# Routing of a mixture-of-experts layer: the row table built earlier, and GpSimd as a second engine for block 0's weight splits

## The chip, the cores and the metric

The kernel runs on one core of one Trainium2 chip. The metric is the device time of one execution in microseconds. The core has five engines that run their own instruction streams and wait for each other through semaphores: TensorE (PE; matmul, with its weight loads as PEld), VectorE (DVE), ScalarE (ACT), GpSimd (POOL) and SyncE (SP; it only issues DMAs here). GpSimd issues the indirect DMAs of this kernel.

## What is computed

One layer of a diffusion backbone: two token mixers, then a mixture of experts over 1024 tokens with 16 experts, and a final norm. The change touches the experts' part. Its reference, cut down:

```python
weights = grp_p * top_p / jnp.sum(top_p, axis=-1, keepdims=True)     # two experts for each token
expert = grp * EXPERTS_PER_GROUP + top_i
# assignments sorted by expert, each expert's segment padded to 128 rows: "blocks"
row_tok = jnp.full((n_rows,), n_tok, jnp.int32).at[dest].set(st)      # which token a row holds
row_w = jnp.zeros((n_rows,), jnp.float32).at[dest].set(sw)            # its weight
block_e = jnp.minimum(jnp.searchsorted(pad_end, jnp.arange(n_blocks) * MOE_BLOCK, side='right'), N_EXPERTS - 1)

def expert_block(args):
    xb, e = args
    gate, up = jnp.split(xb @ w_up[e], 2, axis=-1)
    return (jax.nn.silu(gate) * up) @ w_down[e]

y_rows = lax.map(expert_block, (x_rows, block_e)).reshape(n_rows, d)
y = jnp.zeros((n_tok + 1, d), h.dtype).at[row_tok].add(y_rows * row_w[:, None])
```

## The kernel before

`experts` (L2540) first computes the routing, then runs 31 blocks (BLOCKS) of 128 rows. All times below lie in its part of the span, from about 1692 us on.

Products are done in pairs of parts: a 32-bit matrix `raw` is split into `hi` (a rounded copy, made by ScalarE) and `lo` = raw - hi (VectorE, L2948), and a product is three matmuls, hi x hi, lo x hi, hi x lo (L2739 to L2741). An expert's weights come as three pieces of 128x4096 (q = 0, 1 for w_up, q = 2 for w_down), each split in two halves of 128x2048. A piece is loaded by GpSimd with an indirect DMA, `load(b, q)` (L2680), as soon as `lo_done[q]` says that the block before has been split; block 0 always takes expert 0, so its three pieces are loaded by SyncE at the start (L2650). ScalarE makes the hi halves of block 0's pieces 0 and 1 at L2801. VectorE makes the four lo halves at L2948, called as `split_lo(0, 0)` and `split_lo(0, 1)`.

The routing is done by VectorE in small instructions that each wait for the one before (helper `then`). After L2900 to L2909 it knows each assignment's place. For each of the two choices k it makes `hit` (L2913), `in_block` (L2914) and `is_rank` (L2915), which count up the semaphore `places`. TensorE multiplies them into `table_ps` (L2725): for each row of each block its token. VectorE then makes, in this order:

- the weight parts: `hit` times weight (L2918), and a split into two parts (L2920, L2921), which TensorE multiplies into `h_ps` (L2731): the weight of each row;
- each block's expert: le (L2924), reduce (L2926), min (L2927);
- the row numbers `w_rows` from which the experts' weights are loaded (L2929 to L2935);
- the table of tokens: `filled` (L2937), `row0` (L2938), `table` (L2939), and `target` (L2942), where the results are added.

GpSimd waits for `table` with its first two gathers of rows of x (L2688), then goes on to `load(1, 0)`. TensorE transposes the gathered rows (L2749, `turn_x`), ScalarE makes their hi part (L2814), VectorE the rest (L2953, `x_lo`), and the products of block 0 begin (L2739). VectorE's order behind the routing is `split_lo(0, 0)`, `x_lo(0)`, `split_lo(0, 1)`, then the row weights (L2986, L2987) and the loop over the blocks.

Two more instructions elsewhere serve the prediction as samples. L937 and L2213 are subtractions of GpSimd with two SBUF inputs, the same operation as L2948. L1254 and L1270 are VectorE instructions of a token mixer: L1254 reads a PSUM tile, L1270 two SBUF tiles. L2335 is a VectorE instruction on 8 elements with both inputs in SBUF.

Of the kernel before, what the change touches and what calls it, by code (L numbers as in the profile page):

```python
# [29 lines left out]
P = 128  # L30
# [864 lines left out]
class GateUnits:  # L895
# [21 lines left out]
    def load(self, sp, g):  # L917
        if g >= UNITS:
            return
        if g >= 2:  # L920
            sp.wait_ge(self.lo_done, g - 1)
        col = self.GATE_COLS[g // KD] + g % KD * P
        sp.dma_start(self.raw[:, g % 2, :, :], self.wsrc[:, :, col:col + P]).then_inc(self.w_loaded[g % 2], 16)
# [1616 lines left out]
def experts(nc, m, sem, w):  # L2540
# [10 lines left out]
    with ExitStack() as ctx:  # L2551
# [48 lines left out]
        blk = sb("rt_blk", [P, BLOCKS])  # L2600
        again = sb("rt_again", [P, BLOCKS])
        row0 = sb("rt_row0", [P, BLOCKS])
        part = sb("rt_part", [P, 4])
        filled = sb("rt_filled", [P, BLOCKS])
        spare = lo[:, 2, :]
# [23 lines left out]
            "loaded", "hi_done", "lo_done", "made"))  # L2629
        gathered = [sem(f"ex_gathered{j}") for j in range(2)]  # L2630
        gate_loaded, added, tabled = sem("ex_gate_loaded"), sem("ex_added"), sem("rt_tabled")
        block = ctx.enter_context(nc.Block())

        up_rows = w["w_up"][0].rearrange("e (p h k) n -> (e p h) (k n)", h=2, k=KQ)
# [3 lines left out]
        def each(eng, body):  # L2638

            for b in range(BLOCKS):  # L2640
                body(b, b % 2, b // 2)
        late = lambda b, n: b >= n
        more = lambda b: b < BLOCKS - 1

# [10 lines left out]
        @block.gpsimd  # L2655
        def _(pool):
            pool.iota(rank[:, :], pattern=[[1, P]], base=0, channel_multiplier=0,
                      allow_small_or_imprecise_dtypes=True).then_inc(built, 1)
            pool.iota(token[:, :], pattern=[[P, N]], base=1, channel_multiplier=1,
                      allow_small_or_imprecise_dtypes=True).then_inc(built, 1)  # L2660
            pool.iota(which[:, :], pattern=[[1, WIDE]], base=0, channel_multiplier=0,
                      allow_small_or_imprecise_dtypes=True).then_inc(built, 1)
            pool.iota(rank4[:, :], pattern=[[-1, 4]], base=4, channel_multiplier=0,
                      allow_small_or_imprecise_dtypes=True).then_inc(built, 1)
            pool.memset(ones16[:, :], 1.0).then_inc(built, 1)
            pool.memset(again_n[:, :, 0:1], 0.0).then_inc(built, 1)
            pool.memset(again_n[:, :, 1:N], 1.0).then_inc(built, 1)
            pool.iota(part[:, 0:2], pattern=[[1, 2]], base=0, channel_multiplier=2,
                      allow_small_or_imprecise_dtypes=True).then_inc(part_built, 1)
            pool.iota(part[:, 2:3], pattern=[[0, 1]], base=0, channel_multiplier=1,  # L2670
                      allow_small_or_imprecise_dtypes=True).then_inc(part_built, 1)
            pool.iota(part[:, 3:4], pattern=[[0, 1]], base=SEQ, channel_multiplier=1,
                      allow_small_or_imprecise_dtypes=True).then_inc(part_built, 1)
            pool.memset(again[:, :], 0.0).then_inc(part_built, 1)

            def load(b, q):

                pool.wait_ge(lo_done[q], 2 * b)
                rows = EXPERTS * P * (1 if q == 2 else 2)
                pool.indirect_dma_start(out=raw[:, q, :], out_offset=None, in_=sources[q],  # L2680
                                        in_offset=bass.IndirectOffsetOnAxis(ap=w_rows[:, q, b:b + 1], axis=0),
                                        bounds_check=rows - 1, oob_is_err=False).then_inc(loaded[q], 16)

            def gather(b):
                pool.wait_ge(tabled, 1)
                if b >= 2:
                    pool.wait_ge(s["t_x"], b - 1)
                pool.indirect_dma_start(out=xg[:, b % 2, :], out_offset=None, in_=m.h2,  # L2688
                                        in_offset=bass.IndirectOffsetOnAxis(ap=table[:, b:b + 1], axis=0))\
                    .then_inc(gathered[b % 2], 16)  # L2690
            def add(b):

                pool.wait_ge(tabled, 2)
                pool.wait_ge(s["y_left"], b + 1)
                if b:
                    pool.wait_ge(added, 16 * b)
                pool.indirect_dma_start(
                    out=m.x1, out_offset=bass.IndirectOffsetOnAxis(ap=target[:, b:b + 1], axis=0),
                    in_=yo[:, b % 2, :], in_offset=None, compute_op=ALU.add).then_inc(added, 16)
            gather(0)  # L2700
            gather(1)
            for b in range(BLOCKS):
                if b + 1 < BLOCKS:
                    load(b + 1, 0)
                    load(b + 1, 1)
                if b:
                    load(b, 2)
                if b + 2 < BLOCKS:
                    gather(b + 2)
                if b >= 2:  # L2710
                    add(b - 2)
            add(BLOCKS - 2)
            add(BLOCKS - 1)
            pool.wait_ge(added, 16 * BLOCKS)

        @block.tensor
        def _(pe):
# [7 lines left out]
                    last = pe.matmul(table_ps[:, 0:WIDE], is_rank[:, k, n, :], in_block[:, k, n, :],  # L2725
                                     start=(k == 0 and n == 0), stop=(k == TOP_K - 1 and n == N - 1))
            last.then_inc(tables, 1)
            pe.wait_ge(places, TOP_K + 1)
            for k in range(TOP_K):
                for n in range(N):  # L2730
                    last = pe.matmul(h_ps[:, 0:2 * WIDE], is_rank[:, k, n, :],  # L2731
                                     part_w[:, k, n, :, :].rearrange("p q b -> p (q b)"),
                                     start=(k == 0 and n == 0), stop=(k == TOP_K - 1 and n == N - 1))
            last.then_inc(tables, 1)

            def product(dst, a_hi, a_lo, q, at, k, first, last):

# [5 lines left out]
            def turn_x(b, j, half):  # L2743
                pe.wait_ge(gathered[j], 16 * half + 16)
                if late(b, 1):
                    pe.wait_ge(s["x_lo"], b)
                by_chunk = xg[:, j, :].rearrange("p (c k) -> p k c", k=KD)
                for k in range(KD):
                    last = pe.transpose(x_ps[:, k * P:(k + 1) * P], by_chunk[:, k, :], m.ident[:, :])  # L2749
                last.then_inc(s["t_x"], 1)  # L2750
# [12 lines left out]
            def step(b, j, half):  # L2763
# [21 lines left out]
                    last = pe.transpose(h_ps[:, k * P:(k + 1) * P], by_chunk[:, k, :], m.ident[:, :])  # L2785
                last.then_inc(s["t_h"], 1)
            turn_x(0, 0, 0)
            each(pe, step)
            down(BLOCKS - 1, (BLOCKS - 1) % 2, (BLOCKS - 1) // 2)

# [40 lines left out]
        def _(dve):  # L2831
            count = [0]

            def then(ins):
                count[0] += 1
                ins.then_inc(routed, 1)
                dve.wait_ge(routed, count[0])
# [74 lines left out]
            for k in range(TOP_K):  # L2912
# [1 line left out]
                then(tt(in_block[:, k], hit[:, k], wide(token[:, :], WIDE), ALU.mult))  # L2914
                tt(is_rank[:, k, :, :], wide(where[:, 0, k, :], P), along(rank[:, :], P), ALU.is_equal)\  # L2915
                    .then_inc(places, 1)
            for k in range(TOP_K):
                then(tt(hit[:, k], hit[:, k], wide(weight[:, k, :], WIDE), ALU.mult))  # L2918
            for k in range(TOP_K):
                then(dve.tensor_copy(part_w[:, k, :, 0, :], hit[:, k]))  # L2920
                then(tt(part_w[:, k, :, 1, :], hit[:, k], part_w[:, k, :, 0, :].bitcast(F32), ALU.subtract))  # L2921
            dve.sem_inc(places, 1)
            dve.wait_ge(part_built, 4)
            then(tt(le[:, :, :], ends[:, :].rearrange("p (a e) -> p a e", a=1).to_broadcast([P, BLOCKS, E]),  # L2924
                    which[:, 0:BLOCKS].rearrange("p (b a) -> p b a", a=1).to_broadcast([P, BLOCKS, E]), ALU.is_le))
            then(dve.tensor_reduce(blk[:, :], le[:, :, :], AX.X, ALU.add))  # L2926
            then(ts(blk[:, :], blk[:, :], float(E - 1), None, ALU.min))  # L2927

            then(tt(again[:, 1:], blk[:, 1:], blk[:, 0:BLOCKS - 1], ALU.is_equal))  # L2929
            then(ts(again[:, :], again[:, :], float(SKIP), None, ALU.mult))  # L2930
            for q, rows in enumerate((2 * P, 2 * P, P)):
# [1 line left out]
                    then(dve.scalar_tensor_tensor(out=row0[:, :], in0=blk[:, :], scalar=float(rows), in1=again[:, :],  # L2933
                                                  op0=ALU.mult, op1=ALU.add))
                then(ts(w_rows[:, q, :], row0[:, :], part[:, q:q + 1], None, ALU.add))  # L2935
            dve.wait_ge(tables, 1)
            then(ts(filled[:, :], table_ps[:, 0:BLOCKS], 0.5, None, ALU.is_gt))  # L2937
            then(tt(row0[:, :], table_ps[:, 0:BLOCKS], filled[:, :], ALU.subtract))  # L2938
            dve.tensor_copy(table[:, :], row0[:, :]).then_inc(tabled, 1)  # L2939
            then(ts(filled[:, :], filled[:, :], -1.0, 1.0, ALU.mult, ALU.add))  # L2940
            then(ts(filled[:, :], filled[:, :], part[:, 3:4], None, ALU.mult))
            tt(target[:, :], row0[:, :], filled[:, :], ALU.add).then_inc(tabled, 1)  # L2942

            def split_lo(b, q):
                for h in range(2):
                    at = slice(h * HALF, (h + 1) * HALF)
                    dve.wait_ge(hi_done[q], 2 * b + 1 + h)
                    dve.tensor_tensor(lo[:, q, at], raw[:, q, at], hi[:, q, at].bitcast(F32), ALU.subtract)\  # L2948
                        .then_inc(lo_done[q], 1)
# [13 lines left out]
            def step(b, j, half):  # L2963
# [15 lines left out]
                dve.tensor_tensor(ht_lo[:, :], h_ps[:, :], ht_hi[:, :].bitcast(F32), ALU.subtract)\  # L2979
                    .then_inc(s["h_lo"], 1)  # L2980
                split_lo(b, 2)
            split_lo(0, 0)
            x_lo(0)
            split_lo(0, 1)
            dve.wait_ge(tables, 2)
            then(dve.tensor_copy(row_weight[:, :], h_ps[:, 0:BLOCKS]))  # L2986
            then(tt(row_weight[:, :], row_weight[:, :], h_ps[:, WIDE:WIDE + BLOCKS], ALU.add))  # L2987
# [198 lines left out]
```

## Time and profile before

| | |
|---|---|
| median of 3 runs | 2354.45 us (2353.87 to 2356.31) |
| span of the profiled execution | 2351.6 us |
| busy: PE, PEld, DVE, ACT, POOL | 2150.2, 1736.6, 1410.3, 1025.9, 845.0 us |
| mean granted clock of TensorE | 0.957 |
| weight splits of VectorE (L2948) | 186 instructions, 416.1 us |

The profile lists instructions with their start from the beginning of the span and their duration. An instruction that is issued but can't proceed counts as running, so a duration above that of its like is a wait inside the instruction. Idle time before an instruction is given in brackets with what ended it. The granted clock is the share of full speed that TensorE was allowed; its two levels are 0.50 and 1.00.

### The profile page before, as it was taken

Reading aid. Unit: us, or ns where it says so; the run is one execution under the profiler, and the core shown is the slowest. Engines: PE = TensorE matmul, PEld = TensorE weight load, DVE = VectorE, ACT = ScalarE, POOL = GpSimd, SP = SyncE. Lnnn points to the kernel's source line nnn. Section 1 sums busy time; section 2 is a strip of 40 time slices with the busy share of each in tenths; the row PEclk is TensorE's granted clock in tenths of the full one; section 3 lists DMA queues with packets and bytes.
Section 4 is the critical chain, followed back from the end, with each engine's and each line's share of the span. In section 5 each row is a group of like instructions: output and inputs, shape, how many; then the busy total and the mean of one; then the engine's idle time right before and its main releaser. Section 6 shows DMA issues by size and latency. Waiting matters only on the chain. (4 is left out here: it accounts for less than half of the span.)

```text
span 2351.6 us, 26496 instructions
## 1 busy us (share of the span) xinstructions
PE 2150.2 (91%) x10128; PEld 1736.6 (74%) x10128; DVE 1410.3 (60%) x1688; ACT 1025.9 (44%) x1350; POOL 845.0 (36%) x614
## 2 busy tenths in 40 slices
PE   7999999998898995999999789999789999999992
PEld 1278878887787884888888667777667787877882
DVE  1549541100333324888988546345488899998993
ACT  2332311111234445556655334433246576666762
POOL 6300000111456654567766422210123444543531
PEclk9999999999999997999999999999889999999996
DMA  8733415222654765343554675564379955559425
GB/s 312 239 101 90 124 49 192 85 73 68 225 171 153 186 161 198 96 144 120 159 135 122 174 216 179 175 228 148 153 270 368 366 165 161 167 168 352 119 46 169
DMA packets 267113, 401.36 MB, mean 171 GB/s; under 512 B 30630, under 2 KB 190502, under 8 KB 260204
## 3 DMA queue, kind: packets, MB, share of 16 engines
q1 hardware_dynamic: 237004, 242.34, 32.8%
q0 software_dynamic: 27968, 147.89, 20.1%
q10 hardware_dynamic: 2016, 9.45, 1.1%
q8 instruction: 81, 1.33, 0.2%
q14 instruction: 44, 0.36, 0.0%
HBM read 404.32 MB, written 88.67 MB: 210 GB/s over the span
## 5 line engine op out<-in xcount | busy, mean ns | idle before, releaser
L2948 DVE TENSOR_TENSOR ex_w_lo<-ex_raw,ex_w_hi 128x2048 fp32r<-128x2048 f32 x186 | 416.1, 2284 | 39.1 <-ACT ex_w_hi L2810 38.9
L2810 ACT ACTIVATE ex_w_hi<-ex_raw 128x2048 fp32r<-128x2048 f32 x182 | 337.6, 1909 | 173.9 <-DMA ex_raw<-in_w_up_dram,rt_w_rows 84.9
L861 POOL DMA_DIRECT2D vals<-rows_out x40 | 21.8, 545 | 431.3 <-ACT rows_out L853 431.3
L2680 POOL DMA_INDIRECT ex_raw<-in_w_up_dram,rt_w_rows x60 | 79.7, 1329 | 133.3 <-DVE ex_w_lo L2948 127.2
L2680 POOL DMA_INDIRECT ex_raw<-in_w_down_dram,rt_w_rows x30 | 53.2, 1775 | 184.0 <-DVE ex_w_lo L2948 165.2
L2422 PE MATMUL mo_ps<-mo_branch_hi,mo_w_hi 128*128 128x512 f32 x256 | 105.9, 414 | 8.2 <-POOL mo_branch_lo L2213 4.4
L948 PE MATMUL ml_u_ps<-half_hi,ml_u_w_hi 128*128 128x512 f32 x256 | 106.6, 416 | 6.5 <-ACT ml_u_exp L966 6.5
L948 PE MATMUL gl_u_ps<-half_hi,gl_u_w_hi 128*128 128x512 f32 x256 | 107.7, 421 | 3.2 <-ACT gl_u_exp L966 3.2
L853 ACT ACTIVATE rows_out<-rows_ps 128x512 f32<-128x512 f32 x40 | 24.0, 600 | 198.3 <-PE rows_ps L820 198.3
L2739 PE MATMUL ex_g_ps<-ex_w_hi,ex_x_hi 128*128 128x512 f32 x248 | 103.2, 416 | 6.6 <-DVE ex_x_lo L2953 6.6
L2739 PE MATMUL ex_y_ps<-ex_w_hi,ex_hidden_hi 128*128 128x512 f32 x248 | 100.4, 405 | 7.1 <-DVE ex_w_lo L2948 7.1
L2424 PE MATMUL mo_ps<-mo_branch_lo,mo_w_hi 128*128 128x512 f32 x256 | 102.8, 402 | 0.0
L950 PE MATMUL ml_u_ps<-half_hi,ml_u_w_lo 128*128 128x512 f32 x256 | 102.7, 401 | 0.0
L2423 PE MATMUL mo_ps<-mo_branch_hi,mo_w_lo 128*128 128x512 f32 x256 | 102.6, 401 | 0.0
L949 PE MATMUL ml_u_ps<-half_lo,ml_u_w_hi 128*128 128x512 f32 x256 | 102.6, 401 | 0.0
L2260 DVE TENSOR_TENSOR mo_w_lo<-merge_w,mo_w_hi 128x1024 fp32r<-128x1024 f32 x40 | 49.7, 1243 | 85.9 <-ACT mo_w_hi L2132 85.9
L950 PE MATMUL gl_u_ps<-half_hi,gl_u_w_lo 128*128 128x512 f32 x256 | 100.7, 393 | 0.0
L949 PE MATMUL gl_u_ps<-half_lo,gl_u_w_hi 128*128 128x512 f32 x256 | 100.3, 392 | 0.0
L2740 PE MATMUL ex_g_ps<-ex_w_lo,ex_x_hi 128*128 128x512 f32 x248 | 99.7, 402 | 0.0
L2741 PE MATMUL ex_g_ps<-ex_w_hi,ex_x_lo 128*128 128x512 f32 x248 | 99.2, 400 | 0.0
L971 POOL TENSOR_SCALAR ml_u_exp<-ml_u_exp 128x512 f32<-128x512 f32 x32 | 61.5, 1923 | 102.5 <-ACT ml_u_exp L966 102.4
L2741 PE MATMUL ex_y_ps<-ex_w_hi,ex_hidden_lo 128*128 128x512 f32 x248 | 97.6, 393 | 0.0
(447 smaller groups left out, 6090.8 us busy)
## 6 DMA issues: line engine op xcount, KB each, us to landing
fr_w<-in_w_mod_dram SPq DMA_DIRECT2D x10, 2048.0 KB, 9.9
ml_u_w<-in_w_in_dram SPq DMA_DIRECT2D x32, 512.0 KB, 5.1
gl_u_w<-in_w_in_dram SPq DMA_DIRECT2D x32, 512.0 KB, 5.2
vals<-rows_out POOLq DMA_DIRECT2D x40, 256.0 KB, 2.3
first_values<-vals SPq DMA_DIRECT2D x20, 512.0 KB, 4.5
gl_v<-vals SPq DMA_DIRECT2D x20, 512.0 KB
ml_rows<-scan_rows SPq DMA_DIRECT2D x16, 512.0 KB, 5.7
out_gates<-ml_u_out SPq DMA_DIRECT2D x32, 256.0 KB, 2.5
```

Source lines behind the costliest of these rows:

```text
L948: pe.matmul(self.ps[:, :], a_hi, b_hi, start=(k == 0), stop=False)
L949: pe.matmul(self.ps[:, :], a_hi, b_lo, start=False, stop=False)
L950: last = pe.matmul(self.ps[:, :], a_lo, b_hi, start=False, stop=(k == KD - 1))
L2422: pe.matmul(out, a_hi, b_hi_, start=(k == 0), stop=False)
L2423: pe.matmul(out, a_lo, b_hi_, start=False, stop=False)
L2424: last = pe.matmul(out, a_hi, b_lo_, start=False, stop=(k == KD - 1))
L2680: pool.indirect_dma_start(out=raw[:, q, :], out_offset=None, in_=sources[q], in_offset=bass.IndirectOffsetOnAxis(ap=w_rows[:, q, b:b + 1], ...
L2739: pe.matmul(dst, a_hi[:, ka], hi[:, q, at:at + 512], start=first, stop=False)
L2740: pe.matmul(dst, a_hi[:, ka], lo[:, q, at:at + 512], start=False, stop=False)
L2741: return pe.matmul(dst, a_lo[:, ka], hi[:, q, at:at + 512], start=False, stop=last)
L2810: act.activation(hi[:, q, h], raw[:, q, h], ACT.Copy).then_inc(hi_done[q], 1)
L2948: dve.tensor_tensor(lo[:, q, at], raw[:, q, at], hi[:, q, at].bitcast(F32), ALU.subtract)\
```

## The change

Three things are moved, and one is handed to another engine.

1. VectorE's order. Behind `is_rank` come the experts of the blocks (le, reduce, min), then the table (`filled`, `tokens`, `table`; a tile `rt_tokens` of its own takes the place of `row0`), then the row numbers, then one weight split, `first_low(dve, 0, 1)`, then the weight parts, then `target`. `split_lo(0, 0)` and `split_lo(0, 1)` are gone from behind it.
2. GpSimd makes the other three lo halves of block 0's pieces 0 and 1: one ahead of its first gather, one behind its second gather, one behind `load(1, 0)`. A new semaphore tells it that the row numbers are there.
3. TensorE's product for the row weights stands behind the first transposes.

```diff
+        tokens = sb("rt_tokens", [P, BLOCKS])
+        w_rows_ready = sem("rt_w_rows_ready")
+        def first_low(eng, q, h):
+            at = slice(h * HALF, (h + 1) * HALF)
+            eng.wait_ge(hi_done[q], 1 + h)
+            eng.tensor_tensor(lo[:, q, at], raw[:, q, at], hi[:, q, at].bitcast(F32), ALU.subtract)\
+                .then_inc(lo_done[q], 1)
...
+            first_low(pool, 0, 0)
             gather(0)
             gather(1)
+            first_low(pool, 1, 0)
+            pool.wait_ge(w_rows_ready, 1)
+            load(1, 0)
+            first_low(pool, 1, 1)
             for b in range(BLOCKS):
+                if b:
+                    if b + 1 < BLOCKS:
+                        load(b + 1, 0)
                 if b + 1 < BLOCKS:
-                    load(b + 1, 0)
                     load(b + 1, 1)
...
-            pe.wait_ge(places, TOP_K + 1)
-            for k in range(TOP_K):
-                for n in range(N):
-                    last = pe.matmul(h_ps[:, 0:2 * WIDE], is_rank[:, k, n, :],
...
+            def row_weights():
+                pe.wait_ge(places, TOP_K + 1)
...
             turn_x(0, 0, 0)
+            row_weights()
             each(pe, step)
...
-            for k in range(TOP_K):
-                then(tt(hit[:, k], hit[:, k], wide(weight[:, k, :], WIDE), ALU.mult))
-            for k in range(TOP_K):
-                then(dve.tensor_copy(part_w[:, k, :, 0, :], hit[:, k]))
-                then(tt(part_w[:, k, :, 1, :], hit[:, k], part_w[:, k, :, 0, :].bitcast(F32), ALU.subtract))
-            dve.sem_inc(places, 1)
             dve.wait_ge(part_built, 4)
...
             then(ts(blk[:, :], blk[:, :], float(E - 1), None, ALU.min))
+
+            dve.wait_ge(tables, 1)
+            then(ts(filled[:, :], table_ps[:, 0:BLOCKS], 0.5, None, ALU.is_gt))
+            then(tt(tokens[:, :], table_ps[:, 0:BLOCKS], filled[:, :], ALU.subtract))
+            dve.tensor_copy(table[:, :], tokens[:, :]).then_inc(tabled, 1)
...
-            dve.wait_ge(tables, 1)
-            then(ts(filled[:, :], table_ps[:, 0:BLOCKS], 0.5, None, ALU.is_gt))
-            then(tt(row0[:, :], table_ps[:, 0:BLOCKS], filled[:, :], ALU.subtract))
-            dve.tensor_copy(table[:, :], row0[:, :]).then_inc(tabled, 1)
+            dve.sem_inc(w_rows_ready, 1)
+            first_low(dve, 0, 1)
+            for k in range(TOP_K):
+                then(tt(hit[:, k], hit[:, k], wide(weight[:, k, :], WIDE), ALU.mult))
+            for k in range(TOP_K):
+                then(dve.tensor_copy(part_w[:, k, :, 0, :], hit[:, k]))
+                then(tt(part_w[:, k, :, 1, :], hit[:, k], part_w[:, k, :, 0, :].bitcast(F32), ALU.subtract))
+            dve.sem_inc(places, 1)
...
-            tt(target[:, :], row0[:, :], filled[:, :], ALU.add).then_inc(tabled, 1)
+            tt(target[:, :], tokens[:, :], filled[:, :], ALU.add).then_inc(tabled, 1)
...
-            split_lo(0, 0)
             x_lo(0)
-            split_lo(0, 1)
```

## Rows read from the trace of the kernel before

**Rows 1.** Timeline of VectorE, routing: start us, us, engine, line, operation, tiles

```profile
1702.04 0.29 DVE L2900 TENSOR_TENSOR rt_both<-rt_both,rt_base 128x128 f32<-128x128 f32 x1
```

**Rows 2.** Timeline of VectorE, from the weight parts to x's rest

```profile
1708.43 0.88 DVE L2918 TENSOR_TENSOR rt_hit<-rt_hit,rt_weight 128x256 f32<-128x256 f32 x2
...
1711.02 0.68 DVE L2924 TENSOR_TENSOR rt_le<-rt_ends,rt_which 128x496 f32<-128x496 f32 x1
...
1712.65 0.19 DVE L2929 TENSOR_TENSOR rt_again<-rt_blk 128x30 f32<-128x30 f32 x1
...
1714.37 0.19 DVE L2937 TENSOR_SCALAR rt_filled<-rt_table_ps 128x31 f32<-128x31 f32 x1
...
1714.82 0.18 DVE L2939 CAST rt_table<-rt_row 128x31 int32<-128x31 f32 x1
...
1715.50 4.48 DVE L2948 TENSOR_TENSOR ex_w_lo<-ex_raw,ex_w_hi 128x2048 fp32r<-128x2048 f32 x2
1722.90 1.22 DVE L2953 TENSOR_TENSOR ex_x_lo<-ex_x_ps,ex_x_hi 128x1024 fp32r<-128x1024 f32 x1 [2.91 <-ACT ex_x_hi L2814]
```

**Rows 3.** Timeline of TensorE, second half of the table product to the first expert product

```profile
1708.56 1.89 PE L2725 MATMUL rt_table_ps<-ex_w_lo 128*128 128x32 f32 x8 [0.17 <-DVE ex_w_lo L2915]
1710.99 3.62 PE L2731 MATMUL ex_h_ps<-ex_w_lo 128*128 128x64 f32 x16 [0.54 <-DVEq L2922]
1719.83 1.97 PE L2749 MATMUL ex_x_ps<-ident,ex_x 128*128 128x128 f32 x8 [5.22 <-DMA ex_x<-moe_in,rt_table]
1724.18 0.79 PE L2739 MATMUL ex_g_ps<-ex_w_hi,ex_x_hi 128*128 128x512 f32 x1 [2.37 <-DVE ex_x_lo L2953]
```

**Rows 4.** Timeline of ScalarE, hi halves of block 0 and of block 1

```profile
1699.98 3.71 ACT L2801 ACTIVATE ex_w_hi<-ex_raw 128x2048 fp32r<-128x2048 f32 x2 [1.65 <-DMA ex_raw<-in_w_up_dram]
...
1731.73 3.72 ACT L2810 ACTIVATE ex_w_hi<-ex_raw 128x2048 fp32r<-128x2048 f32 x2 [8.87 <-PE ex_u_ps L2741]
```

**Rows 5.** Timeline of GpSimd: two gathers, and the loads of block 1

```profile
1715.29 1.09 POOL L2688 DMA_INDIRECT ex_x<-moe_in,rt_table  x1 [21.87 <-DVE rt_table L2939]
1716.68 1.96 POOL L2688 DMA_INDIRECT ex_x<-moe_in,rt_table  x1 [0.30 <-issue]
1720.83 1.02 POOL L2680 DMA_INDIRECT ex_raw<-in_w_up_dram,rt_w_rows  x1 [2.19 <-DVE ex_w_lo L2948]
```

**Rows 6.** TensorE's waits, 1725 to 2310: us in total, times, longest

```profile
PE ex_h_ps L2785 <- DVE ex_hidden L2970: 13.5, 10, 2.3
PE ex_y_ps L2739 <- DVE ex_w_lo L2948: 7.1, 1, 7.1
```

**Rows 7.** GpSimd's subtractions of two sizes: ns least/median/most, first and last start

```profile
L937 POOL TENSOR_TENSOR ml_u_w_lo<-ml_u_w,ml_u_w_hi x32: 2347/2404/2891, 587.1 to 883.9; 128x1024 fp32r<-128x1024 f32 x32
...
L2213 POOL TENSOR_TENSOR mo_branch_lo<-mo_branch,mo_branch_hi x32: 1257/1296/1820, 1351.4 to 1527.7; 128x512 fp32r<-128x512 f32 x32
```

**Rows 8.** Timelines of GpSimd and VectorE where both work at once, earlier stages

```profile
698.85 2.89 POOL L937 TENSOR_TENSOR ml_u_w_lo<-ml_u_w,ml_u_w_hi 128x1024 fp32r<-128x1024 f32 x1
...
699.40 2.90 DVE L1270 TENSOR_TENSOR ml_qi<-qm,ml_rows 128x512 f32<-128x512 f32 x1
...
1418.45 2.54 POOL L2213 TENSOR_TENSOR mo_branch_lo<-mo_branch,mo_branch_hi 128x512 fp32r<-128x512 f32 x2 [4.19 <-ACT mo_branch_hi L2139]
1418.52 1.25 DVE L2335 SCALAR_TENSOR_TENSOR mo_mod<-mo_mod 128x8 f32<-128x8 f32 x1
...
590.37 2.35 POOL L937 TENSOR_TENSOR ml_u_w_lo<-ml_u_w,ml_u_w_hi 128x1024 fp32r<-128x1024 f32 x1 [0.94 <-ACT ml_u_w_hi L931]
...
591.83 0.68 DVE L1254 TENSOR_TENSOR ml_kw<-ml_t_ps,ws_col 128x512 f32<-128x512 f32 x1
```

**Rows 9.** Stretches: us; busy PE, PEld, DVE, ACT, POOL; granted clock, DMA share, GB/s

```profile
1724.00:1728.00 4.00, 3.82 (x9) 3.05 (x10) 4.00 (x3) 0.00 (x0) 0.00 (x0) 0.51 0.97 414
1728.00:1732.00 4.00, 4.00 (x19) 3.29 (x19) 0.81 (x3) 0.27 (x1) 1.95 (x2) 1.00 0.31 70
1740.00:1800.00 60.00, 57.48 (x266) 47.22 (x267) 54.86 (x35) 40.36 (x27) 23.50 (x15) 1.00 0.93 351
```

More of the change, by code:

```diff
@@ L2727, in _ @@
             last.then_inc(tables, 1)
-            pe.wait_ge(places, TOP_K + 1)
-            for k in range(TOP_K):
-                for n in range(N):
-                    last = pe.matmul(h_ps[:, 0:2 * WIDE], is_rank[:, k, n, :],
-                                     part_w[:, k, n, :, :].rearrange("p q b -> p (q b)"),
-                                     start=(k == 0 and n == 0), stop=(k == TOP_K - 1 and n == N - 1))
-            last.then_inc(tables, 1)
+            def row_weights():
+                pe.wait_ge(places, TOP_K + 1)
+                for k in range(TOP_K):
+                    for n in range(N):
+                        last = pe.matmul(h_ps[:, 0:2 * WIDE], is_rank[:, k, n, :],
+                                         part_w[:, k, n, :, :].rearrange("p q b -> p (q b)"),
+                                         start=(k == 0 and n == 0), stop=(k == TOP_K - 1 and n == N - 1))
+                last.then_inc(tables, 1)
             def product(dst, a_hi, a_lo, q, at, k, first, last):
@@ L2935, in _ @@
                 then(ts(w_rows[:, q, :], row0[:, :], part[:, q:q + 1], None, ALU.add))
-            dve.wait_ge(tables, 1)
-            then(ts(filled[:, :], table_ps[:, 0:BLOCKS], 0.5, None, ALU.is_gt))
-            then(tt(row0[:, :], table_ps[:, 0:BLOCKS], filled[:, :], ALU.subtract))
-            dve.tensor_copy(table[:, :], row0[:, :]).then_inc(tabled, 1)
+            dve.sem_inc(w_rows_ready, 1)
+            first_low(dve, 0, 1)
+            for k in range(TOP_K):
+                then(tt(hit[:, k], hit[:, k], wide(weight[:, k, :], WIDE), ALU.mult))
+            for k in range(TOP_K):
+                then(dve.tensor_copy(part_w[:, k, :, 0, :], hit[:, k]))
+                then(tt(part_w[:, k, :, 1, :], hit[:, k], part_w[:, k, :, 0, :].bitcast(F32), ALU.subtract))
+            dve.sem_inc(places, 1)
             then(ts(filled[:, :], filled[:, :], -1.0, 1.0, ALU.mult, ALU.add))
             then(ts(filled[:, :], filled[:, :], part[:, 3:4], None, ALU.mult))
-            tt(target[:, :], row0[:, :], filled[:, :], ALU.add).then_inc(tabled, 1)
+            tt(target[:, :], tokens[:, :], filled[:, :], ALU.add).then_inc(tabled, 1)
             def split_lo(b, q):
```

## The prediction

> **What bounds the kernel now.** I read the timelines of the routing engine by engine, then the start of the expert loop, then TensorE's waits over the loop. The routing is one chain of small VectorE instructions, each waiting for the one before [rows 1, 2]; TensorE has little to do there. The table of rows comes late: the weight parts (1708.43 to 1711.02) and the row numbers (to 1714.37) stand ahead of it, though the table product had ended at 1708.56 + 1.89 = 1710.45 [rows 2, 3]. Behind the table's cast is a fixed path: gather at 1715.29 (0.47 behind the cast's start), transposes at 1719.83 (4.54 later), VectorE's rest of x at 1722.90, first expert product at 1724.18 [rows 2, 3, 5]. From there TensorE sets the pace: its two longest groups of waits come to 13.5 + 7.1 = 20.6 us in 585 [rows 6]. So the end moves by about what the first product moves, and the question is when it starts.
>
> **The reordering alone.** The group of le, reduce and min takes 1712.65 - 1711.02 = 1.63 [rows 2]. At 1708.43 it ends at 1710.06, before the table product's 1710.45. With 0.15 for the hand-over (my estimate; on this chain one instruction follows another within 0.04) and 1714.82 - 1714.37 = 0.45 up to the cast, the cast starts at 1711.05 and the gather at 1711.52 instead of 1715.29: 3.8 won. Transposes 1716.06, VectorE's rest of x 3.07 later with 1.2 of its own: 1720.3. But TensorE now does the weight product, 3.62 [rows 3], behind the transposes, and its inputs must be there: VectorE takes 1714.37 - 1712.65 = 1.72 for the row numbers, 2.24 for its own split and 1711.02 - 1708.43 = 2.59 for the weight parts [rows 2], so 1711.1 + 6.55 = 1717.7, and the product ends at 1721.4. First expert product about 1721.6: 2.6 earlier. That is the change's worth if GpSimd's splits cost VectorE nothing.
>
> **GpSimd's splits: their own time.** One is 128x2048 with two SBUF inputs. The same operation takes 2347 ns at the least on 128x1024, 1257 on 128x512 [rows 7]: 2.13 ns for an element more, so 2.347 + 2.18 = 4.5 us (twice the 1024 is 4.7, the other bound). VectorE does one in 2.24 (two in 4.48) [rows 2].
>
> **GpSimd's splits: what they do to VectorE.** Rows 8 show both engines at once. VectorE's L1270, 128x512 with two SBUF inputs, started at 699.40 under a GpSimd subtraction that ended at 698.85 + 2.89 = 701.74, and took 2.90: it ended 0.56 behind GpSimd, 0.56 being what 512 elements take. At 1418.52 a VectorE instruction on 8 elements took 1.25, up to the end of the first of two GpSimd subtractions. But L1254, with one input in PSUM, kept its 0.68 under one [rows 8]. So a VectorE instruction with two SBUF inputs waits for the whole of GpSimd's. The Trainium skill says the same in SBUF — State Buffer, "Who interferes with whom": such an instruction contends with a GpSimd one that reads SBUF, and the later one "fully blocks". This rule speaks against the change, and the trace agrees (2.90 for L1270); without it the sum is the 2.6 won above.
>
> Now the three splits in their places.
> *Hold 1.* The first waits only for ScalarE's first half piece, 1699.98 + 1.86 = 1701.84 [rows 4], so it starts at about 1701.95. VectorE's next, L2900 at 1702.04 [rows 1], has two SBUF inputs and waits until about 1706.5. Everything behind it is a chain and moves by 4.3 (4.5 less what the start overlaps; 4.5 if it slips in one instruction later). The table's cast goes to 1711.05 + 4.3 = 1715.35, the gather to 1715.8: the 3.8 are gone and 0.5 more. The row numbers end at 1717.2, VectorE's own split at 1719.4.
> *Hold 2.* GpSimd issues gather 0 to 1716.9 and gather 1 from 1717.2. An issue takes 1.02 beside an idle VectorE (1720.83), but gather 1 took 1.96 beside VectorE's splits and ended 0.89 behind the one that was running (1715.50 + 2.24) [rows 2, 5]. Here VectorE's split starts at the same moment. Either gather 1 ends at 1718.2 and the second GpSimd split takes over from VectorE's at 1719.4 (case B), or it ends at 1720.3 and the split starts inside the weight parts (case A). Both hold VectorE for 4.4. The skill's same section lets a tensor_tensor leave descriptor generation alone; by that rule it is case B, by the 1.96 of rows 5 it can be A.
> *Hold 3.* Behind the second split GpSimd issues load(1, 0), 1.0 to 1.4, and starts the third at once. In B that is near 1725.3, with VectorE in the last of the weight parts: held to 1729.8, they end at 1730.3, the weight product takes 1730.4 to 1734.0, and the first expert product comes at 1734.1, 9.9 late; x's rest, done by 1732.3, hides. In A it starts at 1726.5, just behind the weight parts (1726.2). The weight product ends at 1730.0, but the instruction for target (L2942, two SBUF inputs) stands ahead of x's rest and is held to 1731.0; x's rest ends at 1732.3, first product 1732.4, 8.2 late.
>
> TensorE's clock: before, the granted clock was 0.51 in 1724 to 1728 and 1.00 behind that, so it rose some 3.8 behind the first expert product [rows 3, 9]; the weight product, 11 us before, had not lifted it. I take the same delay; half of it again at the low level instead of the high (1.9 x 0.5) is the 0.9 that A may lose more. So A is 8.2 to 9.1, B is 9.9, and I take 9.3.
>
> **What follows.** load(1, 0) goes from 1720.83 to about 1725, load(1, 1) to about 1731 [rows 5]. ScalarE wants the first only when the first piece's matmuls are done (before: 1731.73, having waited for TensorE, rows 4), now at 1741: 16 us of cover for a transfer, so nothing. Each later load waits for a split that waits for TensorE, and moves with it. DMA is then nearly full (share 0.93 in 1740 to 1800, rows 9), but that stretch begins with load(2, 0), which moves too; nothing is given back. Where TensorE stalls there its clock may drop or not by chance; for one such drop I keep 3.4 us at half clock, 1.7, either way, as my estimate from the 3.8 above. The other edits (one more semaphore, rt_tokens as a tile of its own) cost under 0.1: they are small instructions at most, and the semaphore has been raised before GpSimd asks.
>
> **Sum.** Profiled span 2351.6 + 9.3 = 2360.9. The median of the runs, 2354.45, is 2.85 above that span; with the same distance 2363.7.
>
> **Rivals.** (1) *The third split misses the chain.* If it starts behind L2942, which is over 2.1 behind the end of the second (one issue takes 1.0 to 1.4), x's rest is free, the weight product ends at 1730.0 and the first product is 5.8 late: 2360.2. For it: an issue of 1.96 beside VectorE's split. Against: VectorE has only short instructions then. Chance 0.10.
> (2) *Not slower: the engines run side by side.* Place: L2900 at 1702. It decides if the first split does not hold it, say because a broadcast input doesn't count as a second SBUF input. Then the first product comes at 1721.6: -2.6, 2351.8; with the first piece's matmuls at full clock (19 in 4.00, rows 9, so 24 in 5.1 instead of 1731.73 - 1724.18 = 7.5) down to -5.0, 2349.5. Against: the holds of rows 8, one with 8 elements. Chance 0.08.
> (3) *The shift is partly absorbed.* Loads (1, 0) and (1, 1) are early against their use, and full DMA engines leave the blocks something to catch up, half of 9.3: 2359.1. For it: share 0.93. Against: the buffers are freed by TensorE's progress. Chance 0.08.
> Forecast: 0.74.
>
> **Range and chances.** The forecast's own range: 8.2 - 1.7 = 6.5 to 9.9 + 1.7 + 0.6 (the 4.7 bound for three splits) = 12.2, so 2361 to 2366.7. With rival (1) and half of (3): 2359.0 to 2367.0. A measurement of this kernel tells about 0.2%, 4.7 us, from no change. Slower: forecast, (1), part of (3): 0.87; within: the rest of (3), most of (2): 0.10; faster 0.03.
>
> **What would show it.** Right: L2900 at 1702 takes some 4.5 instead of 0.29 and ends with GpSimd's first split; the first gather starts at 1715 to 1716.5; two more VectorE instructions take over 3 us before a first expert product at 1732 to 1734.5. Wrong: L2900 keeps 0.29 and the gather starts near 1711.5 (rival 2); first product near 1730 (rival 1); first product 9 late and an end only 4 to 5 late (rival 3).

## The result, and the profile after

| | before | changed |
|---|---|---|
| median of 5 runs | 2353.87 us (2344.55 to 2356.31) | 2369.03 us (2360.88 to 2371.04) |
| ratio, with 95% interval | 1 | 1.0064 (1.0047 to 1.0081) |
| span of the profiled execution | 2351.6 us | 2367.3 us |

The changed kernel is slower by 15.2 us (11.1 to 19.1 by the interval), and that is above the top of the predicted range, 2367.0. Its profiled span is 15.7 longer. Four instants divide it: the routing's first instruction, VectorE's first product of gate and up in block 0 and in block 30 (`ex_hidden<-ex_u_ps`), and the end.

| stretch, us | before | changed | difference |
|---|---|---|---|
| up to the routing's first instruction | 1692.36 | 1693.18 | +0.82 |
| from there to block 0's hidden | 45.83 | 56.67 | +10.84 |
| block 0's hidden to block 30's | 556.32 | 560.30 | +3.98 |
| from there to the end of the span | 57.09 | 57.15 | +0.06 |

The first line lies ahead of all that is changed, and repeated executions differ there by some us either way (the routing of the fourteen profiles in this document starts at 1687.0 to 1695.4). So I count from the routing's first instruction. Two things are left: +10.84 in the routing and block 0, and +3.98 in a loop whose instructions nobody changed.

The routing first. VectorE's timeline of the changed kernel (start, us, engine, line, operation, tiles), of which I keep the cast to the table, VectorE's own split and the instructions out of line:

```profile
1702.86 4.52 DVE L2918 TENSOR_TENSOR rt_both<-rt_both,rt_base 128x128 f32<-128x128 f32 x1
...
1716.06 0.18 DVE L2944 CAST rt_table<-rt_tokens 128x31 int32<-128x31 f32 x1
...
1717.98 2.29 DVE L2648 TENSOR_TENSOR ex_w_lo<-ex_raw,ex_w_hi 128x2048 fp32r<-128x2048 f32 x1
1720.19 5.19 DVE L2956 TENSOR_TENSOR rt_hit<-rt_hit,rt_weight 128x256 f32<-128x256 f32 x2
1725.42 5.10 DVE L2958 CAST ex_w_lo<-rt_hit 128x256 fp32r<-128x256 f32 x1
...
1731.01 0.29 DVE L2958 CAST ex_w_lo<-rt_hit 128x256 fp32r<-128x256 f32 x1
...
1732.63 1.21 DVE L2974 TENSOR_TENSOR ex_x_lo<-ex_x_ps,ex_x_hi 128x1024 fp32r<-128x1024 f32 x1
```

And GpSimd's in the same stretch:

```profile
1702.71 4.51 POOL L2648 TENSOR_TENSOR ex_w_lo<-ex_raw,ex_w_hi 128x2048 fp32r<-128x2048 f32 x1 [8.47 <-ACT ex_w_hi L2819]
1716.53 1.11 POOL L2696 DMA_INDIRECT ex_x<-moe_in,rt_table  x1 [9.31 <-DVE rt_table L2944]
1717.95 0.96 POOL L2696 DMA_INDIRECT ex_x<-moe_in,rt_table  x1 [0.30 <-issue]
1718.91 5.73 POOL L2648 TENSOR_TENSOR ex_w_lo<-ex_raw,ex_w_hi 128x2048 fp32r<-128x2048 f32 x1
1724.80 1.03 POOL L2688 DMA_INDIRECT ex_raw<-in_w_up_dram,rt_w_rows  x1 [0.15 <-issue]
1725.85 4.50 POOL L2648 TENSOR_TENSOR ex_w_lo<-ex_raw,ex_w_hi 128x2048 fp32r<-128x2048 f32 x1
```

Laid side by side the three holds can be read off. `rt_both`, 0.29 before [rows 1], takes 4.52 and ends at 1707.38, 0.16 behind GpSimd's split. The weight parts' products, 0.88 before [rows 2], take 5.19 and end at 1725.38; here it is GpSimd that waited first, for VectorE's split to end at 1720.27, which makes its own 5.73 instead of 4.51. The cast L2958 takes 5.10, its twin at 1731.01 takes 0.29. The holds are 4.23, 4.31 and 4.81. TensorE's and ScalarE's lines show what they did to block 0 (TensorE's transposes, weight product and first expert product; the last line is ScalarE's first hi half of block 1, released by the end of the first piece's matmuls):

```profile
1721.26 1.97 PE L2766 MATMUL ex_x_ps<-ident,ex_x 128*128 128x128 f32 x8 [5.76 <-DMA ex_x<-moe_in,rt_table]
1731.88 3.62 PE L2748 MATMUL ex_h_ps<-ex_w_lo 128*128 128x64 f32 x16 [8.64 <-DVEq L2960]
1735.31 0.77 PE L2756 MATMUL ex_g_ps<-ex_w_hi,ex_x_hi 128*128 128x512 f32 x1
```

```profile
1743.38 3.72 ACT L2828 ACTIVATE ex_w_hi<-ex_raw 128x2048 fp32r<-128x2048 f32 x2 [19.09 <-PE ex_u_ps L2758]
```

The first expert product begins 42.13 behind the routing's first instruction; before it was 31.82 [rows 3]. That is +10.3. ScalarE's half follows at +10.8, counted in the same way [rows 4]. The 0.5 between them is TensorE's clock:

```profile
1738.00:1740.00 2.00, 2.00 (x6) 1.59 (x5) 0.00 (x0) 0.00 (x0) 0.00 (x0) 0.50 0.82 336
1740.00:1744.00 4.00, 4.00 (x18) 3.24 (x18) 0.00 (x0) 0.62 (x1) 0.00 (x0) 1.00 0.00 0
```

The granted clock (third number from the right) stays at 0.50 (1.2 GHz) until 1740, 4.7 behind the first expert product, against 3.8 before [rows 9]. At half speed the 0.9 more costs some 0.45.

Now the loop. These are groups of TensorE's matmuls by line in 1760 to 2290 (count | busy us, mean ns of one | idle us), and the stretch as a whole (busy PE, PEld, DVE, ACT, POOL, clock, DMA share, GB/s); first before, then changed:

```profile
L2739 PE MATMUL ex_u_ps<-ex_w_hi,ex_x_hi 128*128 128x512 f32 x228 | 88.7, 389 | 0.0
...
1760.00:2290.00 530.00, 513.88 (x2375) 425.41 (x2375) 495.61 (x313) 352.90 (x226) 230.10 (x138) 0.99 0.66 215
```

```profile
L2756 PE MATMUL ex_u_ps<-ex_w_hi,ex_x_hi 128*128 128x512 f32 x226 | 89.2, 395 | 0.0
...
1760.00:2290.00 530.00, 518.95 (x2361) 422.55 (x2360) 493.75 (x311) 352.44 (x226) 225.69 (x140) 0.99 0.67 221
```

At the same granted clock, 0.99, one matmul of one shape takes 395 ns instead of 389. The distance from the start of one matmul to the start of the next tells it better: 233.1 ns instead of 227.6 (mean over 1760 to 2290 of the expert products' distances between 180 and 300 ns, some 1900 of them). The same instructions are 2.4% slower, though the change touches none of them. Matmuls of the earlier stages keep their distance: 229.7 in both kernels over 100 to 500 us.

### The profile page after: what moved, and what is told of

The parts are those of the page before. It is cut to its first block and busy times, and to the rows that moved or that the text cites. A ratio compares the mean times of both kernels' runs of the same rounds, so it can differ in the third digit from the quotient of the medians.

```text
span 2367.3 us, 26498 instructions
## 1 busy us (share of the span) xinstructions
PE 2162.4 (91%) x10128; PEld 1739.1 (73%) x10128; DVE 1419.9 (60%) x1685; ACT 1026.1 (43%) x1350; POOL 853.0 (36%) x617
## 5 line engine op out<-in xcount | busy, mean ns | idle before, releaser
L2969 DVE TENSOR_TENSOR ex_w_lo<-ex_raw,ex_w_hi 128x2048 fp32r<-128x2048 f32 x182 | 407.3, 2285 | 45.9 <-ACT ex_w_hi L2828 42.3
L2757 PE MATMUL ex_y_ps<-ex_w_lo,ex_hidden_hi 128*128 128x512 f32 x248 | 98.6, 398 | 0.0
```

Of the source, the lines that this page charges most:

```text
L2757: pe.matmul(dst, a_hi[:, ka], lo[:, q, at:at + 512], start=False, stop=False)
```

## The experiments

I had one theory, that the splits on GpSimd hold VectorE and that block 0 starts later by the sum, and two rivals for the excess over the prediction: that a late start costs more than itself in the loop, and that the loop is slower for a reason of its own. A diff is against the changed kernel or the kernel before, as said. The interval behind a ratio is the 95% one. All start times are counted from the routing's first instruction of the same profile, and compared with before.

**1. The changed kernel again.** No edit.

> The changed kernel once more, on the chip of the runs below. Theory (three holds of VectorE by GpSimd's splits, and nothing else): the first expert product is 10.3 us late against the kernel before, and the end as well, so a ratio of 1.0044 to 1.0050. Rival (the expert loop makes a late start longer): 15 us late at the end, ratio 1.0064, with the excess growing over the blocks.

Measured: 1.0071 (1.0056 to 1.0087). First expert product +10.3, block 0's hidden to block 30's 560.08. Both parts are there again. One detail moved: GpSimd's first split came one instruction later in VectorE's chain, and held the next one for as long:

```profile
1701.75 4.62 DVE L2920 TENSOR_TENSOR rt_prod<-rt_hots,rt_both 128x256 f32<-128x256 f32 x1
```

**2. The order alone, and one split of the three.** Against the changed kernel; in the second, only the last two splits go back to VectorE:

```diff
-            first_low(pool, 0, 0)
...
-            first_low(pool, 1, 0)
...
-            first_low(pool, 1, 1)
...
             dve.sem_inc(w_rows_ready, 1)
+            first_low(dve, 0, 0)
             first_low(dve, 0, 1)
...
             x_lo(0)
+            first_low(dve, 1, 0)
+            first_low(dve, 1, 1)
```

> The change's order, but all four lo halves are made by VectorE: (0,0) and (0,1) ahead of the weight parts, (1,0) and (1,1) behind x's rest. Theory (the holds are the whole cost): the first gather starts at about 1711.5 in the frame of the kernel before, no VectorE instruction of the routing takes over 2.4 us, the first expert product is at 1723.7, 0.5 earlier than before, and the time is within 1 us of the kernel before. Rival (the reordering, with the weight product behind the transposes, costs by itself): still 5 us or more slower.

> GpSimd makes only the first of the three lo halves, VectorE the rest. Theory: only hold 1 is left: the routing's L2918 takes 4.5 us, the gather starts at 1715.8 in the frame of before, the first expert product at about 1725.6, so the end is 1.4 us later than before, 9 us earlier than the changed kernel. Rival (the first hold is the costly one, since the whole routing chain is behind it): 4 us or more slower than before.

Measured: without any split on GpSimd 1.0015 (1.0002 to 1.0028), with the first alone 1.0028 (1.0015 to 1.0040). With none, the first gather is 3.8 earlier than before and the first product 0.6 earlier:

```profile
1708.80 1.09 POOL L2696 DMA_INDIRECT ex_x<-moe_in,rt_table  x1 [18.08 <-DVE rt_table L2941]
```

With one, the first product is 1.4 later: the hold, 4.2, less the 2.24 of VectorE's split that it saves, is 2.0 worse than -0.6. The second and third hold were not taken out one at a time, but the sum of the rows comes out nearly right: -0.6 for the order, less 2.2 for the split that VectorE is spared ahead of the first product, plus 4.2 + 4.3 + 4.8 makes 10.5, measured 10.3. So the three holds are the cause of the 10.3, and each was paid in full.

The times of the two missed what was expected. The order alone should have won a little and lost 3.5 us (0.5 to 6.6); with the first split it should have lost 1.4 and lost 6.6 (3.5 to 9.4). Something in the order costs that isn't in the routing.

**3. A late start and nothing else.** Against before: six subtractions on VectorE ahead of x's rest, whose result is written again by `split_lo(0, 1)`:

```diff
             split_lo(0, 0)
+            dve.wait_ge(hi_done[1], 1)
+            for _ in range(6):
+                then(tt(lo[:, 1, 0:HALF], raw[:, 1, 0:HALF], hi[:, 1, 0:HALF].bitcast(F32), ALU.subtract))
             x_lo(0)
```

> The kernel before, with six more subtractions of 128x2048 on VectorE (their result is overwritten) between the split of block 0's first piece and x's rest: a bare delay of the first expert product by 11.0 us, and no splits on GpSimd. Theory (a late start is passed on one to one): 11 us slower, ratio 1.0047. Rival (the loop makes a late start longer, by the clock or by the loads): 15 us or more.

Measured: 1.0046 (1.0031 to 1.0060), 10.8 us (7.3 to 14.1), for a first product 11.0 late. That interval alone couldn't tell 11 from 14; the loop does. Block 0's hidden to block 30's is 556.87, against 556.32 before, and not 560. A late start is passed on as it is, neither absorbed nor enlarged, so the other 4 us aren't its consequence.

**4. The tile.** What is left is the new tile `rt_tokens`: 31 numbers in a partition, which with rounding move every tile allocated behind it by 128 bytes (worked out from the sizes; the traces hold no addresses), those of x (`ex_x_hi`, `ex_x_lo`) and of hidden (`ex_hidden_hi`, `ex_hidden_lo`) among them; the tiles of the weights lie ahead and don't move. First the kernel before with an unused tile of that size there:

```diff
         row0 = sb("rt_row0", [P, BLOCKS])
+        tokens = sb("rt_tokens", [P, BLOCKS])
```

> The kernel before, with nothing but an unused tile rt_tokens (31 floats) allocated behind rt_row0, so that every tile behind it lies 128 bytes further on. In the traces of the changed kernel and of the two kernels made from it TensorE's expert matmuls start 0.233 us apart, against 0.2276 in the kernel before and in the bare delay. Theory A (the address of TensorE's operands sets the distance): 0.233 here too, the last two blocks longer by about 3 us, 3 to 5 us slower in all. Theory B (it comes from the order of TensorE's instructions): 0.2276, no change.

Measured: 1.0021 (1.0009 to 1.0033), 4.9 us (2.1 to 7.8), from a tile that nothing reads or writes. The first product is where it was (31.86 against 31.82), and the matmuls take the changed kernel's 395 ns:

```profile
L2740 PE MATMUL ex_u_ps<-ex_w_hi,ex_x_hi 128*128 128x512 f32 x226 | 89.2, 395 | 0.0
```

Then the changed kernel, and that of the order alone, with the tile allocated last, so that nothing moves:

```diff
-        tokens = sb("rt_tokens", [P, BLOCKS])
...
         gate2 = sb("ex_gate2", [P, D])
+        tokens = sb("rt_tokens", [P, BLOCKS])
```

> The changed kernel, with rt_tokens allocated behind ex_gate2, so that all other tiles lie where they lay before. Theory A: matmuls 0.2276 apart, and the time is that of the three holds alone, 10.5 to 11.5 us slower than before (ratio 1.0045 to 1.005). Theory B: 0.233, 15 to 17 us slower.

> The change's order with all four lo halves on VectorE, as in the run without GpSimd's splits, and rt_tokens allocated last. Theory A: first expert product 0.5 to 1 us earlier than in the kernel before and the end too, so a time within 1.5 us of it (that run was 3.5 us slower with the tile in the middle). Theory B: 3 us slower still.

Measured: the changed kernel comes down to 1.0054 (1.0038 to 1.0070) and the order alone to 0.9995 (0.9982 to 1.0008). By time, the changed kernel's gain isn't clear of noise: 12.7 us over before (8.9 to 16.5) instead of 15.2, and the expected ratio was 1.0045 to 1.005. Its profile tells it: block 0's hidden to block 30's is 554.48, against 560.30 and 560.08 in the changed kernel's two. In both the matmuls are back at 389 ns; this is the first one's line:

```profile
L2756 PE MATMUL ex_u_ps<-ex_w_hi,ex_x_hi 128*128 128x512 f32 x228 | 88.7, 389 | 0.0
```

And two other distances, against before, with `rt_pad` of 62 or 16 numbers in place of the unused tile (256 and 64 bytes):

> The kernel before with an unused tile that moves what lies behind it by 256 bytes instead of 128. Theory (only the place of TensorE's stationary operands within a 256-byte pattern counts): matmuls again 0.2276 apart and no change of the time. Rival (any shift off the old place costs): 0.233.

> The same with 64 bytes. Theory: a distance of its own between 0.226 and 0.234; if it is 0.233 the good places repeat less often than every 64 bytes, if 0.2276 the 128-byte shift is the exception. A single time can't tell 3 us; the distance of the matmuls is what is read.

Measured: 256 bytes give 0.9998 (0.9982 to 1.0014) and 389 ns. 64 bytes give 395 ns; that kernel's one time, 2352.91, says nothing, since its routing happened to begin 5.4 early (at 1687.01). The stretch from block 0's hidden to block 30's tells it in every profile:

| moved by, bytes | kernels | hidden to hidden, us | distance of matmuls, ns |
|---|---|---|---|
| 0 | before, delay, tile last (2), late weights (experiment 5), the two of experiment 6 | 554.5 to 557.7 | 227.5 to 227.6 |
| 256 | padded | 555.2 | 227.5 |
| 128 | changed (2), order alone, first split alone, unused tile | 559.8 to 562.2 | 233.1 |
| 64 | padded | 560.8 | 233.4 |

The two kinds don't overlap; their means (8 and 6 profiles) are 556.2 and 560.6, so 4.4 us.

The same rows say which tiles do it. A product of gate or up reads x's parts, which moved, and the weights, which didn't; a product of y reads hidden's parts, which moved, and the weights. Both kinds are slower: 227.4 to 233.1 ns for gate and up, 228.0 to 233.2 for y (before and changed, counted as above; 233.1 and 233.3 with the unused tile). The 128x128 operand that TensorE loads ahead of each matmul, x's parts for the one and hidden's for the other, is the only tile of theirs that moved, so it is both, each for its own products.

In the middle of the loop little of the difference shows. VectorE is busy 494 of 530 us there, and in many blocks it works from one hidden to the next without a gap, before and changed alike 17.5 us. This is such a stretch, of the kernel before; its last four splits go on to 2262, where the next hidden begins:

```profile
2244.57 0.68 DVE L2970 TENSOR_TENSOR ex_hidden<-ex_u_ps,ex_gate 128x512 f32<-128x512 f32 x1
2245.17 1.21 DVE L2953 TENSOR_TENSOR ex_x_lo<-ex_x_ps,ex_x_hi 128x1024 fp32r<-128x1024 f32 x1
2246.30 4.48 DVE L2948 TENSOR_TENSOR ex_w_lo<-ex_raw,ex_w_hi 128x2048 fp32r<-128x2048 f32 x2
...
2253.22 8.89 DVE L2948 TENSOR_TENSOR ex_w_lo<-ex_raw,ex_w_hi 128x2048 fp32r<-128x2048 f32 x4
```

The difference comes mostly at the end: from block 27's hidden to block 30's the first kind takes 49.3 to 50.8 us, the second 52.5 to 53.2. These are the hidden products of blocks 29 and 30, before and changed:

```profile
2279.48 0.68 DVE L2970 TENSOR_TENSOR ex_hidden<-ex_u_ps,ex_gate 128x512 f32<-128x512 f32 x1
...
2294.51 0.69 DVE L2970 TENSOR_TENSOR ex_hidden<-ex_u_ps,ex_gate 128x512 f32<-128x512 f32 x1 [1.90 <-issue]
```

```profile
2293.25 0.69 DVE L2991 TENSOR_TENSOR ex_hidden<-ex_u_ps,ex_gate 128x512 f32<-128x512 f32 x1
...
2310.15 0.69 DVE L2991 TENSOR_TENSOR ex_hidden<-ex_u_ps,ex_gate 128x512 f32<-128x512 f32 x1 [3.06 <-issue]
```

The distance is 15.03 before, 16.90 changed; 16.89 with the unused tile and 14.95 with the tile last.

**5. A version that beats both.** From the order alone with the tile last: x's rest goes ahead of the weight parts on VectorE, and TensorE's product for the row weights goes into block 0's matmuls, into free columns of `table_ps`, from which VectorE reads the row weights during block 0 (that part of the edit isn't shown):

```diff
             first_low(dve, 0, 1)
+            dve.wait_ge(s["x_hi"], 1)
+            dve.tensor_tensor(xt_lo[:, :], x_ps[:, :], xt_hi[:, :].bitcast(F32), ALU.subtract)\
+                .then_inc(s["x_lo"], 1)
+            first_low(dve, 1, 0)
+            first_low(dve, 1, 1)
             for k in range(TOP_K):
...
-                        last = pe.matmul(h_ps[:, 0:2 * WIDE], is_rank[:, k, n, :],
+                        last = pe.matmul(table_ps[:, 2 * WIDE:4 * WIDE], is_rank[:, k, n, :],
...
+                if b == 0:
+                    row_weights()
...
             turn_x(0, 0, 0)
-            row_weights()
```

> A version meant to be faster than both: table first, all lo halves on VectorE, VectorE's weight parts behind x's rest and block 0's splits, TensorE's weight product behind the transposes of block 1's rows, into free columns of the table's bank; rt_tokens allocated last. Theory A with the path of the prediction: gather at 1711.5, x's rest ends at 1720.3 in the frame of before, first expert product 3.8 us earlier, weight product mostly in the pause of TensorE between blocks 0 and 1: 3 to 3.8 us faster (ratio 0.9985). Rival (the weight product on TensorE's path costs its 3.6 us, or the loads set the pace): no gain.

Measured: 0.9976 (0.9966 to 0.9987), 5.6 us faster than before and about 20 than the changed kernel. The first product is 28.09 behind the routing's start, so 3.7 earlier, and nothing stands between it and the transposes but x's parts:

```profile
1717.21 1.97 PE L2763 MATMUL ex_x_ps<-ident,ex_x 128*128 128x128 f32 x8 [5.62 <-DMA ex_x<-moe_in,rt_table]
1721.56 0.79 PE L2753 MATMUL ex_g_ps<-ex_w_hi,ex_x_hi 128*128 128x512 f32 x1 [2.37 <-DVE ex_x_lo L2955]
```

3.7 of the 5.6 is the first product; the rest is within the interval (3.1 to 8.0), and the profile doesn't show it, whose loop is 1.4 longer than before. The two moves were tried together only.

**6. What holds VectorE.** Against before: at the moment of the first split GpSimd writes a tile of the same size, once by a memset (it reads nothing), once by a copy (it reads one tile), and waits for it before the gathers (the diff is the memset's; the other has `pool.tensor_copy(spot, raw[:, 0, 0:HALF])` in its place):

```diff
+            pool.wait_ge(hi_done[0], 1)
+            spot = xg[:, :, :].rearrange("p a d -> p (a d)")
+            pool.memset(spot, 0.0).then_inc(probe, 1)
+            pool.wait_ge(probe, 1)
             gather(0)
```

> The kernel before, with a GpSimd memset of 128x2048 floats (it only writes, into the tile of gathered rows) at the moment of the changed kernel's first split. If a hold needs a GpSimd instruction that reads SBUF, the routing's L2900 keeps its 0.29 us and the gather its 1715.3; if any GpSimd work holds VectorE, L2900 takes as long as the memset, about 2 us.

> The same with a GpSimd copy of 128x2048 floats, one SBUF input. Theory: one input is enough, L2900 is held until the copy's end, 2 us or more. Rival (only GpSimd work with two SBUF inputs holds VectorE): L2900 keeps 0.29 us.

Measured, memset:

```profile
1703.50 1.80 POOL L2703 MEMSET ex_x<- 128x2048 f32 x1 [8.59 <-ACT ex_w_hi L2806]
```

```profile
1703.53 0.29 DVE L2905 TENSOR_TENSOR rt_both<-rt_both,rt_base 128x128 f32<-128x128 f32 x1
1703.86 0.43 DVE L2907 TENSOR_TENSOR rt_prod<-rt_hots,rt_both 128x256 f32<-128x256 f32 x1
1704.32 0.61 DVE L2909 TENSOR_REDUCE rt_dest<-rt_prod 128x16 f32<-128x256 f32 x1
1704.97 0.37 DVE L2910 CAST rt_dest_i<-rt_dest 128x16 int32<-128x16 f32 x1
```

Under a memset VectorE's instructions with two SBUF inputs keep their times. A cast, 0.17 before, took 0.37 and ended with the memset. The copy:

```profile
1705.14 1.99 POOL L2703 COPY ex_x<-ex_raw 128x2048 f32<-128x2048 f32 x1 [8.67 <-ACT ex_w_hi L2806]
```

```profile
1705.42 1.99 DVE L2907 TENSOR_TENSOR rt_prod<-rt_hots,rt_both 128x256 f32<-128x256 f32 x1
```

`rt_both`, where the hold was expected, had begun 0.05 ahead of the copy and kept its 0.29; the next instruction took 1.99 instead of 0.43: one SBUF input of GpSimd's is enough. The Trainium skill, SBUF — State Buffer, "Who interferes with whom", states that a VectorE instruction with two SBUF inputs contends with a GpSimd instruction that reads SBUF and not with one that only writes it. The rows agree (1.99 under the copy, 0.43 under the memset).

The gather did not keep its place, as was expected of the memset's kernel: it began 1.07 behind the table's cast instead of 0.47, why wasn't tried, and so fell inside VectorE's split, where its issue took 2.86 instead of 1.09 (last section). The times of the two kernels, 2359.91 and 2360.84 in one run each, hold this too and aren't the holds' alone.

## Why the prediction was wrong

The forecast was +9.3, its top +12.2; the change costs 15.2. The routing's part came close to the forecast; what put the time above the range is the place of one new tile, which was costed at nothing.

*What bounds the kernel; the end moves as the first product moves.* Right in what was drawn from it: 11.0 late gave 10.8. "From there TensorE sets the pace" is not: in the middle of the loop many blocks are as long as VectorE's work (17.5 us without a gap), and it is at the end that VectorE stands idle for TensorE (3.06 ahead of block 30's hidden, 1.90 before). The short waits of TensorE in [rows 6] don't tell the two apart.

*The reordering alone, gather 3.8 earlier.* Right, 3.8 measured with no split on GpSimd. The first product, forecast 2.6 earlier with VectorE doing one split, was 0.6 earlier with VectorE doing two; the second split is 2.24, so 2.8 for the forecast's case.

*GpSimd's own time, 4.5.* Right, 4.51 and 4.50 where it had not to wait.

*The holds.* Right in kind and nearly in place and size: forecast 4.3, 4.4 and, in case B, some 3.9 (weight parts to 1730.3 instead of 1719.4 + 4.4 + 2.59 = 1726.4), measured 4.2, 4.3 and 4.8, and the gather 0.4 later than before instead of 0.5. Between the cases A and B it was B, as B says: gather 1 took 0.96, the second split took over at the end of VectorE's, and the third fell in the last of the weight parts. B gave 9.9 for the first product, measured 10.3. The difference is in the third hold: it caught the first cast of the weight parts, where I had let it catch the end of them, so that 1.4 us of work were left behind it instead of 0.5. The cast had begun at 1725.42, ahead of the split, while GpSimd was still issuing `load(1, 0)` (1724.80 to 1725.83): by its 0.29 it should have been through before the split, so the issue must already have held it. The run without GpSimd's splits shows such a hold by itself. The second cast takes 0.49 instead of 0.29 and ends 0.09 behind the issue (1715.64 + 1.12 = 1716.76):

```profile
1715.64 1.12 POOL L2688 DMA_INDIRECT ex_raw<-in_w_up_dram,rt_w_rows  x1 [4.47 <-DVE ex_w_lo L2648]
```

```profile
1716.36 0.49 DVE L2956 CAST ex_w_lo<-rt_hit 128x256 fp32r<-128x256 f32 x1
```

It is 0.49 with the same 0.09 in the first split's kernel and in the order with the tile last. The Trainium skill, SBUF — State Buffer, "Who interferes with whom", names cast among the operations that can contend with GpSimd when their operands meet certain conditions. The rows agree that this cast does, and the one under the memset in experiment 6 (0.37 instead of 0.17).

*The choice of 9.3.* A value between A and B that is neither. B's own was 9.9, and its clock term should have stood in it as it did in A's. Measured 10.3 + 0.5 = 10.8. The 0.5 is in part chance: the clock rose 4.7 behind the first expert product here and 4.0 in the repeat, where the term is 0.2. None of this leads out of the predicted range.

*Loads and DMA give nothing back.* Right: the delayed start alone shows no gain, no loss (loop 556.87 against 556.32).

*"The other edits (one more semaphore, rt_tokens as a tile of its own) cost under 0.1: they are small instructions at most."* This is the step that failed. I costed the tile by its instructions, and its cost is its place: 128 bytes that move the tiles of x and hidden, and 2232 matmuls of 128x512 (72 in each of 31 blocks) that take 2.4% more. TensorE's busy time is 2162.4 instead of 2150.2, 12.2 more (2149.0 with the tile last), of which the part outside VectorE's cover reaches the end. Measured alone 4.9 (2.1 to 7.8); in the changed kernel's profile 4.0. With 10.8 this is 14.8 of the profile's 14.9 behind the routing's start. Nothing in the trace of before shows this cost, so it had to be bounded, and I bounded it by a reason instead.

*The rivals.* (1) The third split missing the chain: no. (2) The engines side by side: no, every two-input instruction under a split was held. (3) Part of the shift absorbed: no. The rival that was missing is the one on the other side of (3), a loop that becomes slower by itself.

## What to carry to other kernels

On this chip a subtraction handed to GpSimd isn't a second pair of hands while VectorE walks a chain: each of three held it for the full 4.2 to 4.8 us and spared it 2.24, and only the first one's 2.24 lay ahead of the first product. Move the order, not the work; what gained here was to take the row weights' parts and their product out of the way of block 0. And a tile that is added or resized is part of a change: allocate it behind the operands of the hot matmuls, or pad, and compare the mean of one matmul in a stage that was not touched before any difference is explained.

## What the runs showed of the hardware

- The place in SBUF of the operand that TensorE loads (x's or hidden's parts, the weights unmoved) changes its pace. With it moved by 0 or 256 bytes, a 128x512 matmul of the expert loop follows the last by 227.5 to 227.6 ns; moved by 64 or 128, by 233.1 to 233.4 ns. What in the memory does it wasn't tried, nor other distances.
- An issue of an indirect DMA is held by VectorE's subtraction, and whoever is first has the way. With VectorE's split begun at 1717.20 (the memset's kernel), an issue of a gather that began inside it took until 1 us behind the end of its first half:

```profile
1717.20 4.49 DVE L2953 TENSOR_TENSOR ex_w_lo<-ex_raw,ex_w_hi 128x2048 fp32r<-128x2048 f32 x2
```

```profile
1717.59 2.86 POOL L2689 DMA_INDIRECT ex_x<-moe_in,rt_table  x1 [12.28 <-DVE rt_target L2947]
```

  The changed kernel's gather 1 began at 1717.95, 0.03 ahead of VectorE's split, and took 0.96; the one above began 0.39 behind a split's start. In the prediction this was the doubt between A (the 1.96 of rows 5) and B; which of the two starts first decides in these rows. The Trainium skill, SBUF — State Buffer, "Who interferes with whom", lets a tensor_tensor leave descriptor generation alone; the 1.96 and 2.86 don't agree with it, and the measurement decides. It is no chance of one gather: behind 1690 in the kernel before, 68 of GpSimd's 152 indirect issues begin inside a split of VectorE's (over 0.05 behind its start, over 0.25 ahead of its end); they take 1.75 at the least and 2.28 in the median, the other 84 0.99 in the median. These issues take their row numbers from a tile in SBUF; whether that is the difference wasn't tried.
- A waiting engine gets its turn between two instructions of the other: GpSimd's second split waited 1.2 us (5.73 instead of 4.51) and took over at the end of VectorE's split, though VectorE's next instruction (L2956) had been issued without a gap.
